# The last query tile turned on TensorE, and y weighted on VectorE, in a two-layer hybrid block

## The chip, the core and the metric

The kernel runs on one core of a Trainium2 chip. The time is the time on the device in microseconds, the median of the runs of one program. The engines of a core work through queues of their own and meet at semaphores: TensorE (PE, with its weight loads as PEld), VectorE (DVE), ScalarE (ACT), GpSimd (POOL), and SyncE (SP), which only issues DMAs here.

## The reference

Two blocks follow each other over 256 tokens of width 1024, each with two layers; all arithmetic is in fp32. The change touches the first block's layers. In one such layer the normalised input is multiplied by a wide matrix, and its columns are cut into z, x, B, C, dt, q, k, v and two gates. A state-space mixer makes y from x, B, C and dt; a windowed attention takes q (three patterns of eight heads), k and v; both results go through a matrix of their own and are gated and added.

```python
y = ssd_chunked(xs, dt, a, bm, cm) + d_skip.astype(f32)[:, None] * xs
y = y.reshape(bsz, s, SSD_INNER) * jax.nn.silu(z.astype(f32))
yg = y.reshape(bsz, s, SSD_GROUPS, SSD_INNER // SSD_GROUPS)
yg = yg * lax.rsqrt(jnp.mean(yg * yg, axis=-1, keepdims=True) + RMS_EPS)
return (yg.reshape(bsz, s, SSD_INNER) * norm_w.astype(f32)).astype(z.dtype)
...
q = apply_partial_rope(q.reshape(bsz, s, ATTN_N_PAT, ATTN_KV_HEADS, ATTN_HEAD_DIM), cos, sin)
k = apply_partial_rope(k.reshape(bsz, s, ATTN_KV_HEADS, ATTN_HEAD_DIM), cos, sin)
...
scores = jnp.einsum("brhnqe,brhnke->brhnqk", qb, kb, preferred_element_type=jnp.float32) * (dh ** -0.5)
...
merged = (jax.nn.sigmoid(g_ssd) * (y_ssd @ w_ssd_branch[layer])
          + jax.nn.sigmoid(g_attn) * (y_attn @ w_attn_branch[layer]))
```

## The kernel before

**Products.** fp32 weights are split into a high part (`WH`, rounded by ScalarE, line 1170) and a low part (`WL`, the difference, by VectorE, line 1694, the helper `tt` of every VectorE sum, difference and product of two tiles). The activations are split likewise (`uH`, `uL` and `bH`, `bL`). A product is then three matmuls, high by high, high by low and low by high (lines 673 to 675, or 927 to 929 where the result is wanted with columns on the partitions).

**Chunks.** Weights come in chunks of 128 x 2048 in a ring of three buffers. A layer of the first block has one list of chunks: 0 to 47 are the 24 tiles of the wide matrix, two chunks each (tile i has chunks 2i and 2i + 1), then come the branch matrices. A tile of 512 columns takes 24 matmuls a chunk. Every engine has a loop over the chunk number c, and all other work is hung into these loops by hand: "if c == ...". So each engine has a fixed order, and a number c stands for a different moment on each: ScalarE and VectorE split chunk c when TensorE has finished chunk c - 3, so their turn c is at about the time of TensorE's chunk c - 2. In front of its chunk c TensorE runs the small work of turn c (the function `before`).

**Turning the q and k tiles.** The tiles k0, q0, q2, q4, k1, q1, q3, q5 (tiles 3, 7, 10, 13, 17, 19, 20, 21) come out with tokens on the partitions and are wanted with the head's elements there. ScalarE takes the tile out of PSUM into `ev[...]` (line 1298), VectorE applies the rope (turn 2i + 5), POOL lays the upper and lower halves of the words apart (line 1651), SP issues a DMA transpose of 2-byte elements (line 578), and ScalarE merges the halves again into `qT` or `kT` (line 1315, two instructions, at the turns `QK_MERGE`). The semaphore `qk_out` counts finished tiles. TensorE waits for four of them before the scores of heads 0 to 3 (turns 36 to 42) and for all eight before those of heads 4 to 7 (from turn 48, line 814).

**The heads.** Head n has its scores at turn `HEAD_AT[n]` on TensorE (banks 4 to 6), mask, exponentials and normalisation on VectorE and ScalarE two and three turns on, a DMA turn of the probabilities, and the product with the values at turn `HEAD_AT[n] + 4` (lines 711 and 712, bank 7 for heads 0 to 5). ScalarE takes the high part out of bank 7 (line 1356) and VectorE the low part, which raises `o_ready`, both at turn `HEAD_AT[n] + 6`. For head 3 these turns are 42, 46 and 48.

**The y groups.** y comes in four groups of 512 columns, from the x tiles 2, 5, 8 and 11. For group g with x tile i: TensorE turns the conv tile at turn 2i + 5 (line 678, eight transposes), which waits for the convolution's silu and for the last sum of y of the group before (`ssd_y`); y is finished, gated and scaled at turns 2i + 11 to 2i + 13; POOL, a DMA transpose and POOL again turn it; and at turn 2i + 16 it is weighted with the norm's columns and split: ScalarE writes four high parts (line 1350, scaled by a column), VectorE four low parts (line 1958). `xpad` and `conv` are the tiles of the convolution, whose twelve steps on VectorE have line 1780; the turns of its two halves are 2i + 4 and 2i + 5. `EM` (the profile calls it ssd_decay) holds the decay masks, `scratch` is the large region that holds qT, y, ev and most else.

Of the kernel before, what the change touches and what calls it, by code (L numbers as in the profile page):

```python
# [16 lines left out]
F32 = mybir.dt.float32  # L17
# [126 lines left out]
def build(nc, stream, pars, const1, const2, onehot, relb, final_g, ple_g, w_x, out, rev):  # L144
    ctx = ExitStack()
    with ctx:
# [63 lines left out]
        def words(name, at_col, shape):  # L210
# [33 lines left out]
                   words("qk_halves6", BTOK_AT, [2 * T * 512])[:, :], words("qk_halves7", BTOK_AT + 1024, [2 * T * 512])[:, :]]  # L244
# [3 lines left out]
                   early("qk_turned6", 1, 20, 2 * T * 512, U16)[:, :], early("qk_turned7", 0, 20, 2 * T * 512, U16)[:, :]]  # L248
# [128 lines left out]
        words_split = signal("words_split", 8 + GROUPS)  # L377
        words_turned = [signal("words_turned0", 16 * 6), signal("words_turned1", 16 * 6)]
# [34 lines left out]
        y_high = signal("y_high", GROUPS)  # L413
# [30 lines left out]
        y_scaled = signal("y_scaled", GROUPS)  # L444
        conv_done = signal("conv_done", 6)
# [80 lines left out]
        QK_SPLIT = (12, 20, 26, 32, 42, 44, 46, 47)  # L526
        QK_TURN, Y_TURN = (0, 2, 4, 6, 8, 9, 10, 11), (1, 3, 5, 7)
        QK_MERGE = (14, 24, 30, 34, 46, 47, 48, 49)
        CONV_AT = 4
        Y_HIGH, Y_LOW = 16, 16  # L530
# [140 lines left out]
        def _(pe):  # L671
# [42 lines left out]
            def before(l, c):  # L714
# [78 lines left out]
                for g, i in enumerate(XT):  # L793
# [8 lines left out]
                    if c == 2 * i + 10:  # L802
                        pe.wait_ge(ssd_exp.sem, ssd_exp.at(l, 2 * g + 2))
                        nc.tensor.matmul(ps[:, 7, :], BC[:, 4 + g, tok(1)], state, start=True, stop=True).then_inc(off_ps.sem, 1)  # L804
                for n, s in enumerate(HEAD_AT):
# [353 lines left out]
        def _(act):  # L1159
# [32 lines left out]
            for l in range(L):  # L1192
# [39 lines left out]
                for c in range(4, CHUNKS1):  # L1232
# [73 lines left out]
                    for n in range(8):  # L1306
                        if c == QK_MERGE[n]:
# [10 lines left out]
                            ins.then_inc(qk_out.sem, 1)  # L1318
                    for g, i in enumerate(XT):
# [26 lines left out]
                        if c == 2 * i + Y_HIGH:  # L1346
                            act.wait_ge(y_whole.sem, y_whole.at(l, g + 1))
                            for j in range(4):
                                jj = 4 * g + j
                                ins = nc.scalar.activation(bH[:, jj, :].rearrange("p (t n) -> p t n", t=T), Y[g % 2][:, :, tok(j)],  # L1350
                                                           ACT.Identity, scale=par[:, C_SN + jj:C_SN + jj + 1])
                            ins.then_inc(y_high.sem, 1)
# [251 lines left out]
        def _(pool):  # L1604
# [6 lines left out]
            for l in range(L):  # L1611
# [7 lines left out]
                def lay_apart(n):  # L1619

                    pool.wait_ge(att_p.sem, att_p.at(l, n + 1))
                    if n == 4:
                        pool.wait_ge(qk_out.sem, qk_out.at(l, 8))
# [13 lines left out]
                for n in range(8):  # L1637
# [6 lines left out]
                    if 5 <= n < 7:  # L1644
                        lay_apart(n - 3)
# [3 lines left out]
                    if n >= 6:  # L1649
                        pool.wait_ge(qk_out.sem, qk_out.at(l, n - 1))  # L1650
                    nc.gpsimd.tensor_copy(qk_half[n].rearrange("p (h n) -> p h n", h=2),
                                          words_of(ev[QK[n][2]]).rearrange("p n h -> p h n")).then_inc(words_split.sem, 1)
                    if n < GROUPS:
                        g, m = n, Y_TURN[n]
                        pool.wait_ge(y_scaled.sem, y_scaled.at(l, g + 1))
                        if g == 2:
# [5 lines left out]
                                              y_back[g].rearrange("p (h m) -> p h m", h=2)).then_inc(y_whole.sem, 1)  # L1662
                for n in range(4, 7):
                    lay_apart(n)
                    put_together(n)
# [24 lines left out]
        def _(dve):  # L1690
# [102 lines left out]
            for l in range(L):  # L1793
# [49 lines left out]
                for c in range(4, CHUNKS1):  # L1843
# [67 lines left out]
                    for g, i in enumerate(XT):  # L1911
# [32 lines left out]
                        if c == 2 * i + 13:  # L1944
# [4 lines left out]
                            ins.then_inc(y_scaled.sem, 1)  # L1949
                    for n, i in enumerate((0, 1) + XT):  # L1950
                        if c in (2 * i + CONV_AT, 2 * i + CONV_AT + 1):
                            convolve(l, n, c - 2 * i - CONV_AT)
                    for g, i in enumerate(XT):
                        if c == 2 * i + Y_LOW:
                            dve.wait_ge(y_high.sem, y_high.at(l, g + 1))
                            for j in range(4):
                                jj = 4 * g + j
                                ins = nc.vector.scalar_tensor_tensor(
                                    out=bL[:, jj, :].rearrange("p (t n) -> p t n", t=T), in0=Y[g % 2][:, :, tok(j)],
# [431 lines left out]
```

## Time and profile before

| | |
|---|---|
| median of 3 runs | 1525.48 us (1525.25 to 1525.74) |
| profiled execution | 1525.48 us |
| its span | 1523.7 us |
| busy: TensorE matmuls, VectorE, ScalarE, POOL | 1508.5, 1039.7, 926.4, 179.9 us |
| DMA | 288.08 MB, 189 GB/s on the mean |

The span reaches from the first to the last instruction of the profile; the execution is 1.78 us longer. Matmuls overlap, so a row of x8 shows the time from the first's start to the last's end, and starts are what is to be compared. A number in square brackets behind a row is idle time in front of it and what ended it. Times of rows are from the start of the span, and unless it is said otherwise they lie in the first of the two layers of the first block, which begins at 0; the second one repeats it from about 596 us on.

### The profile page before, as it was taken

Reading aid. Unit: us, or ns where it says so; the run is one execution under the profiler, and the core shown is the slowest. Engines: PE = TensorE matmul, PEld = TensorE weight load, DVE = VectorE, ACT = ScalarE, POOL = GpSimd, SP = SyncE. Lnnn points to the kernel's source line nnn. Section 1 sums busy time; section 2 is a strip of 40 time slices with the busy share of each in tenths; the row PEclk is TensorE's granted clock in tenths of the full one; section 3 lists DMA queues with packets and bytes.
Section 4 is the critical chain, followed back from the end, with each engine's and each line's share of the span. In section 5 each row is a group of like instructions: output and inputs, shape, how many; then the busy total and the mean of one; then the engine's idle time right before and its main releaser. Section 6 shows DMA issues by size and latency. Waiting matters only on the chain.

```text
span 1523.7 us, 18981 instructions
## 1 busy us (share of the span) xinstructions
PE 1508.5 (99%) x7612; PEld 1276.1 (84%) x7612; DVE 1039.7 (68%) x1324; ACT 926.4 (61%) x1118; POOL 179.9 (12%) x115
## 2 busy tenths in 40 slices
PE   7999999999999999999999999999999999999998
PEld 7888888888888888988888888888888878888887
DVE  6978876756665555787887775665545676677665
ACT  5766787574355553667778565436555565666564
POOL 1001121422000100001102231100010020002000
PEclk9999999999999999999999999999999999999999
DMA  7456655775456774445556685537767584448541
GB/s 275 166 166 181 194 183 185 203 215 175 167 199 212 204 235 173 171 164 181 177 181 196 189 223 185 169 138 242 221 166 254 212 256 169 149 148 246 174 152 65
DMA packets 132399, 288.08 MB, mean 189 GB/s; under 512 B 97079, under 2 KB 98008, under 8 KB 101848
## 3 DMA queue, kind: packets, MB, share of 16 engines
q1 hardware_dynamic: 131208, 284.44, 58.6%
q10 hardware_dynamic: 1104, 2.43, 0.5%
q8 instruction: 60, 0.98, 0.3%
q14 instruction: 27, 0.22, 0.0%
HBM read 261.69 MB, written 1.84 MB: 173 GB/s over the span
## 4 chain that ended last, share of the span: by engine, by line
PE 93%; DVE 5%; ACT 1%; issue 1%; DMA 0%; SPq 0%; ACTq 0%; DVEq 0%
PE ps L673 25%; PE ps L675 25%; PE ps L674 25%; PE ps L678 2%; PE ps L927 2%; PE ps L928 2%; PE ps L929 2%; DVE w_low L1694 2%; PE ps L799 2%; PE ps L814 1%; DVE conv L1780 1%; PE ps L816 1%; ACT w_high L1170 1%; PE ps L786 0%; PE ps L804 0%
## 5 line engine op out<-in xcount | busy, mean ns | idle before, releaser
L1694 DVE TENSOR_TENSOR w_low<-w_raw,w_high 128x2048 fp32r<-128x2048 f32 (+1 forms) x250 | 574.7, 2299 | 369.0 <-ACT w_high L1170 302.0
L673 PE MATMUL ps<-w_high,u_high 128*128 128x512 f32 x1376 | 547.4, 398 | 0.5 <-DVE w_low L1694 0.5
L675 PE MATMUL ps<-w_high,u_low 128*128 128x512 f32 x1376 | 536.8, 390 | 0.0
L674 PE MATMUL ps<-w_low,u_high 128*128 128x512 f32 x1376 | 535.9, 389 | 0.0
L1170 ACT ACTIVATE w_high<-w_raw 128x2048 fp32r<-128x2048 f32 (+1 forms) x196 | 369.2, 1884 | 260.0 <-PE ps L675 246.8
L673 PEld LDWEIGHTS ps<-w_high,u_high 128*128 128x128 f32 x1376 | 258.5, 188 | 55.4 <-issue 2.4
L675 PEld LDWEIGHTS ps<-w_high,u_low 128*128 128x128 f32 x1376 | 258.3, 188 | 55.0
L674 PEld LDWEIGHTS ps<-w_low,u_high 128*128 128x128 f32 x1376 | 258.7, 188 | 53.9 <-issue 2.4
L673 PE MATMUL ps<-w_high,b_high 128*128 128x512 f32 x384 | 151.5, 395 | 0.0
L675 PE MATMUL ps<-w_high,b_low 128*128 128x512 f32 x384 | 149.7, 390 | 0.0
L674 PE MATMUL ps<-w_low,b_high 128*128 128x512 f32 x384 | 149.5, 389 | 0.0
L1418 ACT ACTIVATE w_high<-w_raw 128x2048 fp32r<-128x2048 f32 x50 | 95.3, 1910 | 45.8 <-PE ps L675 45.6
L927 PE MATMUL ps<-u_high,w_high 128*128 128x256 f32 x384 | 112.8, 294 | 4.2 <-DVE w_low L1694 3.9
L928 PE MATMUL ps<-u_low,w_high 128*128 128x256 f32 x384 | 109.3, 285 | 0.0
L929 PE MATMUL ps<-u_high,w_low 128*128 128x256 f32 x384 | 109.2, 284 | 0.0
L1694 DVE TENSOR_TENSOR scratch<-scratch 128x128 f32<-128x128 f32 (+3 forms) x156 | 68.3, 471 | 34.5 <-ACT scratch L1361 27.1
L675 PEld LDWEIGHTS ps<-w_high,b_low 128*128 128x128 f32 x384 | 72.1, 188 | 15.2
L674 PEld LDWEIGHTS ps<-w_low,b_high 128*128 128x128 f32 x384 | 72.2, 188 | 14.4
L673 PEld LDWEIGHTS ps<-w_high,b_high 128*128 128x128 f32 x384 | 72.1, 188 | 14.3
L927 PEld LDWEIGHTS ps<-u_high,w_high 128*128 128x128 f32 x384 | 74.3, 194 | 6.7 <-DVE w_low L1694 4.3
L928 PEld LDWEIGHTS ps<-u_low,w_high 128*128 128x128 f32 x384 | 74.3, 194 | 1.7 <-issue 1.4
L929 PEld LDWEIGHTS ps<-u_high,w_low 128*128 128x128 f32 x384 | 74.3, 193 | 0.0
(241 smaller groups left out, 1513.1 us busy)
## 6 DMA issues: line engine op xcount, KB each, us to landing
w_raw<-in_stream SPq DMA_DIRECT2D x238, 1024.0 KB, 4.9
w_raw<-in_stream SPq DMA_DIRECT2D x12, 512.0 KB, 4.1
par<-in_pars SPq DMA_DIRECT2D x4, 269.0 KB, 5.2
h<-in_x SPq DMA_DIRECT2D x4, 256.0 KB, 4.9
ple_gain<-in_ple_g ACTq DMA_DIRECT2D x2, 512.0 KB, 5.6
out<-h SPq DMA_DIRECT2D x4, 256.0 KB, 2.1
scratch<-in_const SPq DMA_DIRECT2D x1, 768.0 KB, 7.6
rev<-scratch ACTq DMA_DIRECT2D x1, 768.0 KB, 3.6
```

The lines of the kernel that those rows point to most:

```text
L673: nc.tensor.matmul(o, hi, whi, start=start, stop=False, **kw)
L674: nc.tensor.matmul(o, hi, wlo, start=False, stop=False, **kw)
L675: return nc.tensor.matmul(o, lo, whi, start=False, stop=stop, **kw)
L678: return nc.tensor.transpose(o, i, ident)
L799: last = nc.tensor.matmul(ps[:, 4 + t, e * HD:(e + 1) * HD], EM[t][:, e, :], xdt[:, t, e * HD:(e + 1) * HD], start=True, stop=True)
L814: nc.tensor.matmul(ps[:, 4 + g // 2, (g % 2) * S:(g % 2 + 1) * S], qT[:, g, hh, tok(1)], kT[:, hh, :], start=True, stop=True)
L927: nc.tensor.matmul(o, WH[:, slot, w], uH[:, kk, :], start=first, stop=False, skip_group_check=True)
L928: nc.tensor.matmul(o, WH[:, slot, w], uL[:, kk, :], start=False, stop=False, skip_group_check=True)
L929: last = nc.tensor.matmul(o, WL[:, slot, w], uH[:, kk, :], start=False, stop=kk == KD - 1, skip_group_check=True)
L1170: nc.scalar.activation(WH[:, c % RING, 0:n], W[:, c % RING, 0:n], ACT.Copy).then_inc(high_ready, 1)
L1418: nc.scalar.activation(WH[:, n % RING, :], W[:, n % RING, :], ACT.Copy).then_inc(high_ready, 1)
L1694: return nc.vector.tensor_tensor(out=o, in0=a, in1=b, op=op)
```

## The change

Two edits. First, q5, the last of the eight tiles, isn't turned by POOL, DMA and merge any more. TensorE turns it in front of chunk 47 (`QK_LAST`) with eight fp32 transposes into banks 6 and 7, and ScalarE copies both banks into `qT` at turn 49, in the place of the last merge. TensorE waits there for the rope of q5 (`roped`) and for the low part of head 3's output (the fourth `o_ready`), since that output lies in bank 7. Second, y is weighted in place by VectorE, token half by token half, then ScalarE copies the half to `bH` (rounding it) and VectorE subtracts it into `bL`. This stands ahead of the mask products and of the next convolution's first half in VectorE's turn; the old low parts stood behind them.

```diff
-        QK_SPLIT = (12, 20, 26, 32, 42, 44, 46, 47)
-        QK_TURN, Y_TURN = (0, 2, 4, 6, 8, 9, 10, 11), (1, 3, 5, 7)
-        QK_MERGE = (14, 24, 30, 34, 46, 47, 48, 49)
+        QK_SPLIT = (12, 20, 26, 32, 42, 44, 46)
+        QK_TURN, Y_TURN = (0, 2, 4, 6, 8, 9, 10), (1, 3, 5, 7)
+        QK_MERGE = (14, 24, 30, 34, 46, 47, 48)
+        QK_LAST = 47
         CONV_AT = 4
-        Y_HIGH, Y_LOW = 16, 16
+        Y_WEIGH = 16
...
+                if c == QK_LAST:
+                    pe.wait_ge(roped.sem, roped.at(l, 8))
+                    pe.wait_ge(o_ready.sem, o_ready.at(l, 4))
+                    for hh in range(4):
+                        for t in range(T):
+                            last = turn(ps[:, 6 + hh // 2, (hh % 2) * S + t * P:(hh % 2) * S + (t + 1) * P], ev[QK[7][2]][:, t, tok(hh)])
+                    last.then_inc(qk_ps.sem, 1)
...
-                    for n in range(8):
+                    for n in range(7):
                         if c == QK_MERGE[n]:
...
+                    if c == 49:
+                        act.wait_ge(qk_ps.sem, qk_ps.at(l, 1))
+                        nc.scalar.activation(qT[:, 2], ps[:, 6:8, :].rearrange("p b (j s) -> p (b j) s", j=2), ACT.Copy)\
+                            .then_inc(qk_out.sem, 1)
...
-                        if c == 2 * i + Y_HIGH:
-                            act.wait_ge(y_whole.sem, y_whole.at(l, g + 1))
-                            for j in range(4):
-                                jj = 4 * g + j
-                                ins = nc.scalar.activation(bH[:, jj, :].rearrange("p (t n) -> p t n", t=T), Y[g % 2][:, :, tok(j)],
-                                                           ACT.Identity, scale=par[:, C_SN + jj:C_SN + jj + 1])
-                            ins.then_inc(y_high.sem, 1)
+                        if c == 2 * i + Y_WEIGH:
+                            for t in range(T):
+                                act.wait_ge(y_weighted.sem, y_weighted.at(l, 2 * g + t + 1))
+                                nc.scalar.activation(bH[:, 4 * g:4 * g + 4, tok(t)], four(Y[g % 2][:, t, :]), ACT.Copy)\
+                                    .then_inc(y_high.sem, 1)
...
                     if n == 4:
-                        pool.wait_ge(qk_out.sem, qk_out.at(l, 8))
+                        pool.wait_ge(qk_out.sem, qk_out.at(l, 6))
...
-                for n in range(8):
+                for n in range(7):
...
+                        if c == 2 * i + Y_WEIGH:
+                            dve.wait_ge(y_whole.sem, y_whole.at(l, g + 1))
+                            for t in range(T):
+                                tt(four(y[:, t, :]), four(y[:, t, :]),
+                                   bc(par[:, C_SN + 4 * g:C_SN + 4 * g + 4].unsqueeze(2), 4, P), ALU.mult).then_inc(y_weighted.sem, 1)
+                            for t in range(T):
+                                dve.wait_ge(y_high.sem, y_high.at(l, 2 * g + t + 1))
+                                tt(bL[:, 4 * g:4 * g + 4, tok(t)], four(y[:, t, :]), bH[:, 4 * g:4 * g + 4, tok(t)].bitcast(F32),
+                                   ALU.subtract).then_inc(y_ready.sem, 1)
...
-                    for g, i in enumerate(XT):
-                        if c == 2 * i + Y_LOW:
-                            dve.wait_ge(y_high.sem, y_high.at(l, g + 1))
-                            for j in range(4):
-                                jj = 4 * g + j
-                                ins = nc.vector.scalar_tensor_tensor(
-                                    out=bL[:, jj, :].rearrange("p (t n) -> p t n", t=T), in0=Y[g % 2][:, :, tok(j)],
-                                    scalar=par[:, C_SN + jj:C_SN + jj + 1],
-                                    in1=bH[:, jj, :].bitcast(F32).rearrange("p (t n) -> p t n", t=T), op0=ALU.mult, op1=ALU.subtract)
-                            ins.then_inc(y_ready.sem, 2)
```

VectorE's order at its turn 20 in a layer (the split of chunk 20 to that of chunk 21), before; `tt` has line 1694 in the old file and 1706 in the new one:

```order
L1694 TENSOR_TENSOR w_low<-w_raw,w_high 128x2048
L1937 COPY ssd_decay_57<-scratch 128x8
L1694 TENSOR_TENSOR ssd_decay_57<-ssd_decay_57,scratch 128x8x127
L1694 TENSOR_TENSOR xpad<-ps,rinv_rows 128x4x256
L1958 SCALAR_TENSOR_TENSOR b_low<-scratch,par,b_high 128x256 x4
L1694 TENSOR_TENSOR scratch<-scratch,ps 128x512
L1694 TENSOR_TENSOR w_low<-w_raw,w_high 128x2048
```

The same place in the changed kernel:

```order
L1706 TENSOR_TENSOR w_low<-w_raw,w_high 128x2048
L1706 TENSOR_TENSOR scratch<-scratch,par 128x512 x2
L1706 TENSOR_TENSOR b_low<-scratch,b_high 128x4x128 x2
L1949 COPY ssd_decay_57<-scratch 128x8
L1706 TENSOR_TENSOR ssd_decay_57<-ssd_decay_57,scratch 128x8x127
L1706 TENSOR_TENSOR xpad<-ps,rinv_rows 128x4x256
L1706 TENSOR_TENSOR scratch<-scratch,ps 128x512
```

Two products and two differences now stand in front of the mask products and of xpad; the four low parts behind xpad are gone.

ScalarE's order around its turns 48 and 49, before (line 1315 merges q3 and then q5, line 1356 is the high part of head 3's output):

```order
L1170 ACTIVATE w_high<-w_raw 128x2048
L1298 ACT_TABLE_LOAD
L1298 ACTIVATE scratch<-ps,small 128x512 x2
L1315 ACTIVATE scratch<-qk_turned_80 128x2x4x128 x2
L1356 ACTIVATE b_high<-ps 128x256
L1170 ACTIVATE w_high<-w_raw 128x2048
L1315 ACTIVATE scratch<-qk_turned_81 128x2x4x128 x2
```

And in the changed kernel:

```order
L1180 ACTIVATE w_high<-w_raw 128x2048
L1308 ACT_TABLE_LOAD
L1308 ACTIVATE scratch<-ps,small 128x512 x2
L1325 ACTIVATE scratch<-qk_turned_79 128x2x4x128 x2
L1368 ACTIVATE b_high<-ps 128x256
L1180 ACTIVATE w_high<-w_raw 128x2048
L1331 ACTIVATE scratch<-ps 128x1024
```

The order up to the high part is the same; only the last merge has become a copy out of two banks.

TensorE in front of chunk 47 in the changed kernel, where the old one goes from matmul to matmul:

```order
L678 MATMUL ps<-w_high,u_low 128x512
L681 MATMUL ps<-con,scratch 128x128 x8
L676 MATMUL ps<-w_high,u_high 128x512
L677 MATMUL ps<-w_low,u_high 128x512
```

This is the only row that TensorE has gained in a layer.

## Rows read from the trace of the kernel before

**Rows 1.** The page: busy time of the engines, and the chain that ended last.
```profile
PE 1508.5 (99%) x7612; PEld 1276.1 (84%) x7612; DVE 1039.7 (68%) x1324; ACT 926.4 (61%) x1118; POOL 179.9 (12%) x115
...
PE 93%; DVE 5%; ACT 1%; issue 1%; DMA 0%; SPq 0%; ACTq 0%; DVEq 0%
```

**Rows 2.** Waits of TensorE: total us, times, longest.
```profile
PE ps L678 <- DMA con<-in_const: 3.9, 1, 3.9
```

**Rows 3.** Timeline of TensorE, conv transposes of group 2: start us, length us.
```profile
151.98 1.03 PE L678 MATMUL ps<-con,conv 128*128 128x128 f32 x8
152.77 0.48 PE L673 MATMUL ps<-w_high,u_high 128*128 128x512 f32 x1
153.09 0.40 PE L674 MATMUL ps<-w_low,u_high 128*128 128x512 f32 x1
```

**Rows 4.** TensorE in one stretch: busy (count), granted clock, DMA share, GB/s.
```profile
314.00:319.25 5.25, 5.25 (x24) 1.00 0.92 270
```

**Rows 5.** Timeline of TensorE: the first matmul of chunk 47.
```profile
319.30 0.39 PE L673 MATMUL ps<-w_high,u_high 128*128 128x512 f32 x1
```

**Rows 6.** Timeline of ScalarE at its turn 48.
```profile
313.41 1.91 ACT L1170 ACTIVATE w_high<-w_raw 128x2048 fp32r<-128x2048 f32 x1 [1.05 <-PE ps L675]
315.35 1.28 ACT L1298 ACT_TABLE_LOAD   x1
316.64 1.27 ACT L1298 ACTIVATE scratch<-ps,small 128x512 f32<-128x512 f32 x2
317.80 2.56 ACT L1315 ACTIVATE scratch<-qk_turned 128x1024 uint16<-128x1024 uint16 x2
320.22 0.36 ACT L1356 ACTIVATE b_high<-ps 128x256 fp32r<-128x256 f32 x1
```

**Rows 7.** Timeline of VectorE: end of q5's rope, and head 3's low part.
```profile
313.45 0.49 DVE L1694 TENSOR_TENSOR scratch<-scratch 128x128 f32<-128x128 f32 x2
...
320.61 0.43 DVE L1694 TENSOR_TENSOR b_low<-ps,b_high 128x256 fp32r<-128x256 f32 x1 [2.56 <-ACT b_high L1356]
```

**Rows 8.** Timeline of TensorE: chunk 47 ends, scores of head 4.
```profile
324.51 0.39 PE L675 MATMUL ps<-w_high,u_low 128*128 128x512 f32 x1
324.90 0.70 PE L814 MATMUL ps<-scratch 128*128 128x256 f32 x2
...
325.66 0.60 PE L814 MATMUL ps<-scratch 128*128 128x256 f32 x2
```

**Rows 9.** Timeline of VectorE from its turn 20 to the last sum of y.
```profile
137.53 0.17 DVE L1937 COPY ssd_decay<-scratch 128x8 f32<-128x8 f32 x1
...
139.98 1.67 DVE L1958 SCALAR_TENSOR_TENSOR b_low<-scratch,par,b_high 128x256 fp32r<-128x256 f32 x4
141.58 0.68 DVE L1694 TENSOR_TENSOR scratch<-scratch,ps 128x512 f32<-128x512 f32 x1
...
150.69 0.69 DVE L1694 TENSOR_TENSOR scratch<-scratch 128x512 f32<-128x512 f32 x1
```

**Rows 10.** Groups by form: count, busy us, mean ns, idle before.
```profile
L1694 DVE TENSOR_TENSOR scratch<-scratch 128x512 f32<-128x512 f32 x36 | 24.7, 692 | 6.3 <-ACT scratch L1466 5.2
L1694 DVE TENSOR_TENSOR b_low<-scratch,b_high 128x512 fp32r<-128x512 f32 x22 | 15.1, 684 | 0.0
...
L1407 ACT ACTIVATE b_high<-scratch 128x512 fp32r<-128x512 f32 x22 | 13.5, 614 | 0.0
```

**Rows 11.** Timeline of TensorE in the first 15 us of the run.
```profile
9.75 0.58 PE L927 MATMUL ps<-u_high,w_high 128*128 128x256 f32 x1 [3.85 <-DVE w_low L1694]
...
10.77 0.41 PE L928 MATMUL ps<-u_low,w_high 128*128 128x256 f32 x1
10.98 0.41 PE L929 MATMUL ps<-u_high,w_low 128*128 128x256 f32 x1
...
14.12 0.28 PE L928 MATMUL ps<-u_low,w_high 128*128 128x256 f32 x1
14.23 0.29 PE L929 MATMUL ps<-u_high,w_low 128*128 128x256 f32 x1
```

More of the change, by code:

```diff
@@ L243, in build @@
                    words("qk_halves4", BTOK_AT, [2 * T * 512])[:, :], words("qk_halves5", BTOK_AT + 1024, [2 * T * 512])[:, :],
-                   words("qk_halves6", BTOK_AT, [2 * T * 512])[:, :], words("qk_halves7", BTOK_AT + 1024, [2 * T * 512])[:, :]]
+                   words("qk_halves6", BTOK_AT, [2 * T * 512])[:, :]]
         qk_turn = [early("qk_turned0", 0, 4, 2 * T * 512, U16)[:, :], early("qk_turned1", 1, 4, 2 * T * 512, U16)[:, :],
@@ L247, in build @@
                    early("qk_turned4", 1, 20, 2 * T * 512, U16)[:, :], early("qk_turned5", 0, 20, 2 * T * 512, U16)[:, :],
-                   early("qk_turned6", 1, 20, 2 * T * 512, U16)[:, :], early("qk_turned7", 0, 20, 2 * T * 512, U16)[:, :]]
+                   early("qk_turned6", 1, 20, 2 * T * 512, U16)[:, :]]
         y_half = [words("y_halves0", E_AT, [2 * T * 512])[:, :], words("y_halves1", E_AT, [2 * T * 512])[:, :],
@@ L376, in build @@
         off_ps = signal("off_ps", GROUPS)
-        words_split = signal("words_split", 8 + GROUPS)
-        words_turned = [signal("words_turned0", 16 * 6), signal("words_turned1", 16 * 6)]
+        qk_ps = signal("qk_ps", 1)
+        words_split = signal("words_split", 7 + GROUPS)
+        words_turned = [signal("words_turned0", 16 * 6), signal("words_turned1", 16 * 5)]
         y_whole = signal("y_whole", GROUPS)
@@ L412, in build @@
         group_root = signal("group_root", GROUPS)
-        y_high = signal("y_high", GROUPS)
+        y_high = signal("y_high", 2 * GROUPS)
         qk_out = signal("qk_out", 8)
@@ L444, in build @@
         y_scaled = signal("y_scaled", GROUPS)
+        y_weighted = signal("y_weighted", 2 * GROUPS)
         conv_done = signal("conv_done", 6)
@@ L1643, in _ @@
                         put_together(n - 4)
-                    if 5 <= n < 7:
                         lay_apart(n - 3)
@@ L1648, in _ @@
                         pool.wait_ge(state_out.sem, state_out.at(l, GROUPS))
-                    if n >= 6:
-                        pool.wait_ge(qk_out.sem, qk_out.at(l, n - 1))
+                    if n == 6:
+                        pool.wait_ge(qk_out.sem, qk_out.at(l, 5))
                     nc.gpsimd.tensor_copy(qk_half[n].rearrange("p (h n) -> p h n", h=2),
@@ L1662, in _ @@
                                               y_back[g].rearrange("p (h m) -> p h m", h=2)).then_inc(y_whole.sem, 1)
+                put_together(3)
                 for n in range(4, 7):
```

## The prediction

> **What bounds the kernel now.** I read the busy shares and the chain that ended last first: TensorE is busy for 1508.5 of 1523.7 us, and the chain lies on it for 93% [rows 1]. Then the waits of TensorE alone, to see what it still waits for: the longest are one of 3.9 us for the constants and one of 3.9 us for the first weights [rows 2, 11], both in the first ten microseconds of the run, and nothing in the middle of a layer comes near them. So the rest of the work (ScalarE and VectorE splitting weights, POOL and the DMA turning tiles) is hidden behind matmuls. A saving on those engines is worth nothing by itself. Two things can move the time: instructions added to or taken from TensorE, and a result that now arrives later than TensorE reaches the instruction that wants it. For the second, the places where the change touches a semaphore were read engine by engine in the timeline: the start of chunk 47 and of chunk 48, and the start of chunk 21, each as "when is TensorE there, when is the result there". A chunk of 24 matmuls takes about 5.3 us here: 24 of them lie between 314.00 and 319.25 [rows 4].
>
> **Part 1: eight transposes on TensorE, per layer.** They have the form of the eight that turn a conv tile. Those start at 151.98 and the next matmul starts at 152.77, so eight cost 0.79 us; the matmul behind them is followed by its neighbour after 0.32 us, where 0.23 us is usual (23 steps from 319.30 to 324.51, [rows 5, 8]), which is 0.09 more [rows 3]. 0.88 us a layer, 1.76 us for two. They stand in front of a matmul on the engine that bounds, so nothing hides them. From below 0.79; from above, if they didn't overlap at all: seven starts 0.11 apart and one full length make the 1.03 us of the row, so one is about 0.26 long, and eight of them 2.1 us a layer.
>
> **Part 2: what TensorE waits for in front of them.** The eight write banks 6 and 7, and bank 7 holds the output of head 3 until VectorE has split it, so the code waits for the rope of q5 and for the fourth o_ready. The rope is done at 313.94, long before [rows 7]. The fourth o_ready is the end of the split of head 3, from 320.61 to 321.04. TensorE starts chunk 47 at 319.30 [rows 5], when the 24 matmuls of chunk 46 are issued. VectorE cannot do the split earlier, since it sits idle for 2.6 us until ScalarE has made the high part, and ScalarE works through its queue from 313.41 to 320.58 without a pause: weights of chunk 48, a table load, the tile ga0, the merge of q3, and only then the high part of head 3 [rows 6]. Its first item is released by the end of chunk 45 on TensorE, so this queue doesn't start earlier by being left alone, and the change takes nothing out of it. With 0.03 us from end to start (320.58 to 320.61), TensorE gets going at 321.07 instead of 319.30: 1.77 us. In layer 1 the same two rows stand at the same distance, so one pair is shown for both. A restart after a wait costs about 0.10 more: the first pair of L814, which did wait, took 0.70 us, the next pair 0.60 [rows 8]. So 1.87 us a layer, 3.74 us for two. Before, the same o_ready was wanted only by the value product of head 4 at chunk 52, five chunks later. Behind the waiting transposes stands all of chunk 47, and everything that is released by its matmuls; as TensorE is the bound, that is a shift of the whole program. Bounds: nothing, if ScalarE's queue were 1.8 us shorter in this place; 3.3 us a layer if TensorE had to wait out the whole merge (2.56 us, [rows 6]) once more.
>
> **Part 3: what is given back at chunk 48.** The scores of head 4 waited for the last merge: the last matmul of chunk 47 starts at 324.51, the next should follow after 0.23 us and starts at 324.90, 0.16 us late, and the pair takes 0.10 us more than its neighbour [rows 8]. 0.26 us a layer, 0.52 us for two, goes: the two merges are replaced by one copy of 1024 columns out of PSUM, and a pair of 512 columns each out of PSUM takes 1.27 us [rows 6]. ScalarE is free of the weights of chunk 49 by about 322.4, the transposes end at about 322.1, so q5 is in place at about 323.7, and TensorE reaches the scores at about 327.4. The last DMA turn on the SP queue, POOL's laying apart ahead of it and the waits for both go too; nobody on TensorE waited for them beyond those 0.16 us, so I cost them at nothing. The loads behind them on SP may only come earlier.
>
> **Part 4: the weighting of y.** Before, ScalarE multiplies and rounds (four instructions), and VectorE multiplies again and subtracts at the end of its turn at chunk 20 (four instructions, 139.98 to 141.65, the next from 141.58: 1.60 us) [rows 9]. Now VectorE multiplies (two of 0.69 us), ScalarE copies (two of 0.61), VectorE subtracts (two of 0.68) [rows 10], and this stands at the front of the turn, before the masks of the second half. On VectorE neighbours overlap by about 0.07 (141.65 against 141.58). From 137.53: multiplications end at 138.22 and 138.83, ScalarE's copies at 138.87 and 139.47, the subtractions start at 138.90 and 139.50, and what was next at 137.53 is next at 140.10: 2.57 us later. Taking off the 1.60 us that stood further back leaves +0.97 us. From there to 151.38 VectorE has no pause longer than a hand-over, so the last sum of y, which ends at 151.38 [rows 9], ends at 152.35. TensorE wants it (ssd_y) for the transposes of the next conv tile, which start at 151.98 [rows 3]: 0.60 us of slack, and 0.97 + 0.03 us of delay. 0.40 us late, with the restart 0.50. This happens where y of one group is weighted in the turn in which a conv tile begins: for two of the four groups, in both layers, four times, 2.0 us. The slack reads 0.60 in the other three places too; one of the four stands in the rows. In the turns at chunks 32 and 38 no conv tile follows, and nothing that TensorE takes next from VectorE is as close. Below: 0, if the hand-overs go faster by 0.4 us. Above: 2.57 + 0.03 - 0.60 + 0.10 = 2.1 us each, 8.4 us, if nothing came back from the four instructions that go. I take the worked-out 2.0, with less trust than in parts 1 and 2.
>
> The sum: 1.76 + 3.74 - 0.52 + 2.0 = 7.0 us. The profiled execution took 1525.48 us, 1.78 more than its span, and it equals the median of the three runs, so 1525.5 + 7.0 = 1532.5 us, 0.46% slower. I forecast 1532.4. (A measurement of this kernel can't tell less than about 0.2%, 3 us, from no change.)
>
> **The clock, a rule that speaks against the change.** At the start of the run TensorE had stood still for 3.85 us; the matmuls of 256 columns then followed each other every 0.21 us (1.2 GHz), and from 14.12 on every 0.12 us (2.4 GHz) [rows 11]. So it kept the lower pace for some 4.3 us. In the new kernel the engine stands idle 1.8 us and then only transposes for 0.9 us, twice. If it fell for 4.3 us each time, half the work of that stretch would be lost, 2.1 us a time, 4.3 us in all. The Trainium skill (TensorE: Matmul & The Clock Gate, "HAM oscillation") holds that waits repeated between short bursts of matmuls bring the clock down to half and warns against them, and its part on the PE-mode transpose adds that transposes don't count as activity. No stretch of this trace with such a wait in the middle of dense work shows it either way.
>
> **The rivals.**
> A, the y chain stays hidden: parts 1 to 3 alone, +5.0 us, 1530.5. For it: the slack is 0.60 and my excess 0.40, of hand-overs that I estimate. Against it: VectorE has no idle time on that stretch to take it up.
> B, the y chain costs more: +1 us at each of the four places instead of 0.5, 9.0 us, 1534.5. For it: ScalarE's weights of chunk 21 are now behind its two copies, and the conv tile's first products behind those; against: by the same reckoning each still ends before the step that wants it.
> C, the clock falls in chunk 47: 7.0 + 4.3 = 11.3 us, 1536.8.
> D, not slower: the wait for o_ready is not paid. That is so if ScalarE makes the high part of head 3 by about 318.8; it decides on one number, the 1.77 us. Then 1.76 - 0.52 = 1.2 us remain, with the y chain 3.2; 1526.7 to 1528.7, mostly no change. For it: only if the merge of q3 or the table load went, and both are still in the new order. Faster than before would need a gain of which the waits of TensorE show at most 0.5 us.
>
> **Chances.** The forecast 0.56 (own range 1531.2 to 1534.0), A 0.16, B 0.09, C 0.08, D 0.11. Slower by over 0.2% are the first four (0.89) and a sliver of D, 0.90; within 0.2%: most of D, 0.08; faster: 0.02. The range reaches from just below A to where B ends and C begins: 1529.6 to 1535.8.
>
> **What would show it.** In the new profile: a wait of TensorE at the transposes with scratch for an input, released by VectorE's split of head 3, 1.8 us, twice; behind it eight transposes in 0.8 to 0.9 us; no wait in front of the scores of head 4; a wait of 0.3 to 0.5 us in front of the conv transposes of groups 2 and 3, absent at groups 0 and 1; 16 more matmuls on TensorE and no other change of their count. The sum is wrong if o_ready comes before 319.3 in that stretch, if the y block takes less than 2.2 us on VectorE, or if matmuls behind the wait are spaced like those at the start.

## The result, and the profile after

The changed kernel takes 1533.44 us (1533.17 to 1533.92) against 1525.48 before: slower, ratio 1.0051 with a 95% interval of 1.0038 to 1.0064. Its profiled execution took 1532.54 us with a span of 1530.7, so it stands 7.06 us above the profiled execution of before, where the sum was 7.0. By the medians the difference is 7.96 us; the profiled execution is the fastest of the eight that were taken of the changed kernel, which reach up to 1533.92. The busy shares hardly move; the chain does. The page of the changed kernel, TensorE's busy time and the chain that ended last:

```profile
PE 1510.8 (99%) x7628; PEld 1277.3 (83%) x7628; DVE 1043.2 (68%) x1324; ACT 919.3 (60%) x1100; POOL 178.5 (12%) x113
...
PE 86%; DVE 9%; ACT 3%; issue 1%; DMA 0%; ACTq 0%; DVEq 0%
```

TensorE has the 16 matmuls more that were added, and only 2.3 us more of busy time. But the chain now leaves it for VectorE and ScalarE for 12% of the span, where it was 6% [rows 1]. Which results are late, the waits of TensorE say (total us, times, longest):

```profile
PE ps L681 <- DVE b_low L1706: 3.4, 2, 1.7
PE ps L681 <- DVE scratch L1706: 2.2, 6, 0.4
```

Ahead of them stand only the two of the start of the run, as before [rows 2, 11]. The first here is new, once a layer. The second is the wait of transposes (L681 is `turn`, L678 before) for sums of VectorE; four of its six are new. The first in the timeline of TensorE (start us, length us):

```profile
319.89 0.39 PE L678 MATMUL ps<-w_high,u_low 128*128 128x512 f32 x1
321.98 1.06 PE L681 MATMUL ps<-con,scratch 128*128 128x128 f32 x8 [1.71 <-DVE b_low L1706]
322.80 0.48 PE L676 MATMUL ps<-w_high,u_high 128*128 128x512 f32 x1
323.12 0.39 PE L677 MATMUL ps<-w_low,u_high 128*128 128x512 f32 x1
...
328.13 0.39 PE L678 MATMUL ps<-w_high,u_low 128*128 128x512 f32 x1
328.37 0.59 PE L824 MATMUL ps<-scratch 128*128 128x256 f32 x2
```

From the last matmul of chunk 46 to the first transpose are 2.10 us by the unrounded times, and a step without a wait is 0.23: 1.87 us lost. Of these 1.71 are the lateness of head 3's low part, the rest is the hand-over to TensorE. The transposes occupy 0.82 us, and the matmul behind them is followed by its neighbour after 0.32 us instead of 0.23: 0.91 us. And the scores of head 4 (L824) follow the last matmul after 0.24 us and the pair takes 0.59, where it was 0.39 and 0.70 [rows 8]: 0.26 us given back. ScalarE's queue, which sets the moment of the wait, and VectorE's answer:

```profile
314.23 1.91 ACT L1180 ACTIVATE w_high<-w_raw 128x2048 fp32r<-128x2048 f32 x1 [1.05 <-PE ps L678]
316.16 1.28 ACT L1308 ACT_TABLE_LOAD   x1
317.46 1.27 ACT L1308 ACTIVATE scratch<-ps,small 128x512 f32<-128x512 f32 x2
318.61 2.54 ACT L1325 ACTIVATE scratch<-qk_turned 128x1024 uint16<-128x1024 uint16 x2
321.01 0.37 ACT L1368 ACTIVATE b_high<-ps 128x256 fp32r<-128x256 f32 x1
321.27 1.91 ACT L1180 ACTIVATE w_high<-w_raw 128x2048 fp32r<-128x2048 f32 x1
323.08 1.03 ACT L1331 ACTIVATE scratch<-ps 128x1024 f32<-128x1024 f32 x1
```

```profile
321.41 0.42 DVE L1706 TENSOR_TENSOR b_low<-ps,b_high 128x256 fp32r<-128x256 f32 x1 [2.94 <-ACT b_high L1368]
```

It is the queue of [rows 6] 0.8 us further on, item for item. The copy of q5 out of the two banks (L1331) ends at 324.11, over four microseconds before the scores want it.

The other place, VectorE from its turn 20 to the last sum of y, and TensorE at the conv transposes behind it:

```profile
137.15 1.29 DVE L1706 TENSOR_TENSOR scratch<-scratch,par 128x512 f32<-128x512 f32 x2
138.54 1.30 DVE L1706 TENSOR_TENSOR b_low<-scratch,b_high 128x512 fp32r<-128x512 f32 x2
139.75 0.17 DVE L1949 COPY ssd_decay<-scratch 128x8 f32<-128x8 f32 x1
...
151.33 0.69 DVE L1706 TENSOR_TENSOR scratch<-scratch 128x512 f32<-128x512 f32 x1
```

```profile
151.38 0.39 PE L678 MATMUL ps<-w_high,u_low 128*128 128x512 f32 x1
152.16 1.06 PE L681 MATMUL ps<-con,conv 128*128 128x128 f32 x8 [0.40 <-DVE scratch L1706]
```

The block takes 139.75 - 137.15 = 2.60 us. The turn began 0.38 us earlier on the clock of the run than before (137.15 against 137.53) and its last sum starts 0.64 later (151.33 against 150.69, [rows 9]): 1.02 us of delay. The transposes start 0.79 us behind the last matmul instead of 0.23: 0.56 us. In the transposes themselves 0.03 us more are lost, since the second follows the first after 0.14 us instead of 0.11. The same gap, 0.79, stands at 192.5, 750.9 and 792.0; at group 1 there was nothing to wait for, 0.23 (110.89 to 111.12).

### The profile page after: what moved, and what is told of

It is laid out like the page before. It is cut to its first block, busy times and chain, and to the rows that moved or that the text cites. A ratio compares the mean times of both kernels' runs of the same rounds, so it can differ in the third digit from the quotient of the medians.

```text
span 1530.7 us, 18991 instructions
## 1 busy us (share of the span) xinstructions
PE 1510.8 (99%) x7628; PEld 1277.3 (83%) x7628; DVE 1043.2 (68%) x1324; ACT 919.3 (60%) x1100; POOL 178.5 (12%) x113
## 4 chain that ended last, share of the span: by engine, by line
PE 86%; DVE 9%; ACT 3%; issue 1%; DMA 0%; ACTq 0%; DVEq 0%
PE ps L676 23%; PE ps L678 23%; PE ps L677 23%; DVE w_low L1706 3%; PE ps L681 3%; DVE conv L1792 2%; PE ps L937 2%; PE ps L939 2%; PE ps L938 2%; PE ps L824 1%; DVE scratch L1706 1%; ACT w_high L1180 1%; PE ps L802 1%; PE ps L826 1%; DVE xpad L1706 1%
## 5 line engine op out<-in xcount | busy, mean ns | idle before, releaser
L678 PE MATMUL ps<-w_high,u_low 128*128 128x512 f32 x1376 | 537.0, 390 | 0.0
L678 PEld LDWEIGHTS ps<-w_high,u_low 128*128 128x128 f32 x1376 | 258.3, 188 | 55.1
L678 PE MATMUL ps<-w_high,b_low 128*128 128x512 f32 x384 | 149.8, 390 | 0.0
L678 PEld LDWEIGHTS ps<-w_high,b_low 128*128 128x128 f32 x384 | 72.1, 188 | 15.2
```

Source lines behind the costliest of these rows:

```text
L678: return nc.tensor.matmul(o, lo, whi, start=False, stop=stop, **kw)
```

## How the experiments are read

Since every kernel here issues the same products in the same order, each one's TensorE timeline can be laid over that of before, matmul by matmul. How far it lags behind after each place gives each place's cost in that one execution, apart from the first 23 us, where the profiled executions differ by up to 1.5 us although the kernels don't differ there. All numbers in us, counted from TensorE's first matmul (3.9 to 4.1 us after the span begins); "chunk 47" is the wait, the transposes and what the scores give back. The medians are a second reading beside the places. The two need not agree closely: the intervals of the ratios are 2.6 to 4.7 us wide.

| kernel | first 23 us | conv transposes, 4 places | L802, 2 places | chunk 47, each layer | elsewhere | end | median (runs) | ratio to before |
|---|---|---|---|---|---|---|---|---|
| changed kernel | -0.41 | 0.6, 0.6, 0.6, 0.6 | 0 | 2.52, 2.54 | 0 | +7.05 | 1533.44 (5) | 1.0051 [1.0038, 1.0064] |
| e_first | +0.62 | 0 | 0 | 2.53, 2.53 | 0 | +5.68 | 1532.09 (5) | 1.0038 [1.0025, 1.0050] |
| e_second | +0.21 | 0.6, 0.6, 0.6, 0.6 | 0 | 0, 0 | 0 | +2.62 | 1527.91 (11) | 1.0016 [1.0007, 1.0025] |
| e_banks | -0.22 | 0.6, 0.6, 0.6, 0.6 | 0 | 0.63, 0.63 | 0.12 | +3.56 | 1529.05 (11) | 1.0022 [1.0013, 1.0030] |
| e_late | -0.73 | 0 | 0.53, 0.54 | 2.53, 2.53 | 0 | +5.45 | 1531.51 (5) | 1.0037 [1.0025, 1.0050] |
| e_both | +1.53 | 0 | 0.57, 0.53 | 0.63, 0.63 | 1.62 | +5.55 | 1528.01 (10) | 1.0016 [1.0006, 1.0025] |
| e_twice | -0.64 | 0 | 0.53, 0.59 | 1.50, 1.50 | 1.61 | +5.08 | 1530.54 (7) | 1.0029 [1.0018, 1.0040] |
| e_long | -0.29 | 0.6, 0.6, 0.6, 0.6 | 0 | 8.60, 7.90 | 0 | +18.54 | 1543.09 (4) | 1.0112 [1.0097, 1.0128] |
| e_free | -0.83 | 0 | 0 | 0.63, 0.63 | 0 | +0.54 | 1527.55 (11) | 1.0011 [1.0002, 1.0020] |

The kernel before, run beside them on the same chip, took 1525.48 (with the changed kernel), 1525.60 (e_first, e_second, e_banks, e_both), 1525.84 (e_late, e_twice, e_long) and 1526.24 (e_free); these three groups of experiments ran on three chips. One execution of e_both that took 6656.55 us is left out. In the changed kernel the start hid 0.41 us: its places cost 7.46.

## One edit at a time: e_first and e_second

e_first makes the first edit only. The weighting of y is put back:

```diff
-        Y_WEIGH = 16
+        Y_HIGH, Y_LOW = 16, 16
...
+                        if c == 2 * i + Y_HIGH:
+                            act.wait_ge(y_whole.sem, y_whole.at(l, g + 1))
```

> The first edit alone: q5 is turned on TensorE, y is weighted as before. Theory (the three terms stand by themselves): +5.0 us over the kernel before, of which 3.7 is the wait for head 3's split, 1.8 the transposes, and 0.5 comes back at the scores; the starts at the conv transposes of groups 2 and 3 are 0.23 us behind the matmul before, as before. Rival (the edits act on each other, for instance since POOL and the DMA queue are emptier): the conv transposes still start late, and the whole is 7 to 8 us.

Its waits of TensorE that matter here:

```profile
PE ps L680 <- DVE b_low L1707: 3.4, 2, 1.7
...
PE ps L680 <- DVE scratch L1707: 0.6, 2, 0.3
```

The wait for b_low is whole, the one for the sums of y is back to the 0.6 us of the kernel before. 2.53 us a layer, 5.06 in all, where 5.0 was expected. The medians differ by 6.5 us (by the interval 3.8 to 7.6), 1.4 more than the places of the one profile account for; no run shows where that stands.

e_second makes the second edit only: q5 goes by POOL, DMA and merge again.

```diff
-        QK_MERGE = (14, 24, 30, 34, 46, 47, 48)
-        QK_LAST = 47
+        QK_MERGE = (14, 24, 30, 34, 46, 47, 48, 49)
```

> The second edit alone: y is weighted on VectorE, q5 is turned by DMA as before. Theory: +2.2 us (four times 0.56 us of wait in front of the conv transposes of groups 2 and 3), and the 0.16 us of wait at the scores of head 4 stay. Rival (the y block is hidden and its 2 us come from something that the first edit triggers): within 0.5 us of the kernel before.

```profile
PE ps L679 <- DVE scratch L1693: 2.2, 6, 0.4
```

Of the two new waits only this one is there: 0.6 us at four places, 2.4 us. 5.06 and 2.40 make the 7.46 of the changed kernel, so by the places the two edits act apart from each other, and both cost.

## What the first edit's 2.5 us are: e_banks, e_twice

e_banks puts the transposes into banks 4 and 5. These are free once the scores of head 3 have been masked, long before chunk 47, so TensorE waits for that and not for the output in bank 7 (ScalarE's copy reads banks 4 and 5 too):

```diff
-                    pe.wait_ge(o_ready.sem, o_ready.at(l, 4))
+                    pe.wait_ge(att_masked.sem, att_masked.at(l, 4))
...
-        last = turn(ps[:, 6 + hh // 2, ...
+        last = turn(ps[:, 4 + hh // 2, ...
```

> The changed kernel, with the eight transposes into banks 4 and 5 instead of 6 and 7, so that they wait for the mask of head 3, long done, and not for the split of head 3's output. Theory (bank 7 is what TensorE waits for): 3.7 us less than the changed kernel, +3.3 us over the kernel before; no wait in front of the transposes. Rival (TensorE would wait there for something else that comes as late, or the time goes to the next place where ScalarE is behind): less than 2 us of it comes back.

TensorE, and ScalarE's high part of head 3, in e_banks:

```profile
320.08 0.40 PE L678 MATMUL ps<-w_high,u_low 128*128 128x512 f32 x1
320.32 1.04 PE L681 MATMUL ps<-con,scratch 128*128 128x128 f32 x8
321.11 0.47 PE L676 MATMUL ps<-w_high,u_high 128*128 128x512 f32 x1
```

```profile
321.24 0.37 ACT L1368 ACTIVATE b_high<-ps 128x256 fp32r<-128x256 f32 x1
```

The high part is as late as ever, a microsecond behind the first transpose, and nobody waits. The transposes follow after 0.24 us, occupy 0.79, and the matmul behind them costs 0.09 more. With the 0.26 given back, 0.63 us a layer remain of 2.53; the difference, 1.90, is the wait and the 0.03 us that the first transpose behind it took longer. Both layers show it. (The 0.12 us under "elsewhere" stand at the value products of one head in layer 1.) So the wait comes from the choice of the bank, not from the transposes.

e_twice (the kernel e_both, below, with every transpose of q5 issued twice) sizes the transposes by themselves:

```diff
-                    for hh in range(4):
+                    for hh in tuple(range(4)) * 2:
```

> As the kernel with banks 4 and 5 and the later weighting, but each of the eight transposes is done twice. Theory (a transpose in front of a chunk costs its own 0.11 us of TensorE and nothing else): 8 more in each layer are 0.87 us a layer, +1.75 us over the kernel without the doubling, +3.0 over the kernel before; 16 of them stand in a row 0.11 us apart. Rival (part of the 0.88 us is a fixed price of the switch from one kind of matmul to the other): less than 1.4 us more; or (they don't overlap) 4 us more.

```profile
319.31 1.91 PE L681 MATMUL ps<-con,scratch 128*128 128x128 f32 x16
320.97 0.48 PE L676 MATMUL ps<-w_high,u_high 128*128 128x512 f32 x1
```

Sixteen occupy 1.66 us where eight took 0.79: 0.87 us for eight more, and the place costs 1.50 instead of 0.63. So the doubling costs 1.74 us over both layers, as expected (1.75): in front of chunk 47 the length of the transposes on TensorE is paid in full.

## What the second edit's 2.4 us are: e_late, e_both, e_free

e_late is the changed kernel with the y blocks of groups 0 and 1 two turns later, away from the turn in which a conv tile begins (they stood at 20, 26, 32 and 38):

```diff
-        Y_WEIGH = 16
+        Y_WEIGH = (22, 28, 32, 38)
...
-                        if c == 2 * i + Y_WEIGH:
+                        if c == Y_WEIGH[g]:
```

> The changed kernel, banks 6 and 7 as they are, with groups 0 and 1 of y weighted two turns later (22 and 28 instead of 20 and 26): the same instructions in another place. Theory (it is the place on VectorE's way to the last sum of y that costs): 2.2 us less than the changed kernel, +4.9 over the kernel before, and the conv transposes start 0.23 us behind the matmul before. Rival (the amount of work costs, wherever it stands): the time stays within 0.5 us of the changed kernel's, with the waits in another place.

Its waits of TensorE:

```profile
PE ps L681 <- DVE b_low L1706: 3.4, 2, 1.7
...
PE ps L681 <- DVE scratch L1706: 0.6, 2, 0.3
PE ps L802 <- DVE ssd_decay L1706: 0.5, 2, 0.3
```

The four waits are gone, so they did come from the block's place. But a wait of another kind has come, at the products of xdt with the decay masks, and costs 0.53 us a layer, nearly half of the gain of 1.2; 4.9 us over the kernel before had been expected, and the places add up to 6.1. Why is read on VectorE, POOL and TensorE at turn 32, where the block of group 2 stands, which e_late did not move:

```profile
215.11 3.42 DVE L1706 TENSOR_TENSOR w_low<-w_raw,w_high 128x2048 fp32r<-128x2048 f32 x1 [1.58 <-ACT w_high L1180]
218.46 2.98 DVE L1706 TENSOR_TENSOR scratch<-scratch,par 128x512 f32<-128x512 f32 x2
...
222.81 1.21 DVE L1706 TENSOR_TENSOR ssd_decay<-ssd_decay,scratch 128x1016 f32<-128x1016 f32 x1
```

```profile
216.35 3.94 POOL L1662 COPY qk_halves<-scratch 128x2048 uint16<-128x2048 uint16 x1
```

```profile
224.08 2.00 PE L802 MATMUL ps<-xdt,ssd_decay 128*128 128x64 f32 x16 [0.27 <-DVE ssd_decay L1706]
```

The two products take 2.98 us instead of 1.29: they end 1.14 us after POOL's copy (220.29), so nearly all of their own work lies behind it. The decay mask, which now stands behind the block, is done at 224.02, and TensorE, that was due at 223.65 (0.23 behind the last matmul, which starts at 223.42), starts at 224.08. With the slower restart that is the 0.53. In the changed kernel it came to the same place at 225.10, 1.2 us of that lag from the two waits before, and the mask was there with 0.2 us to spare. One wait had hidden the next.

e_both joins e_banks and e_late.

> The changed kernel with banks 4 and 5, and with groups 0 and 1 of y weighted two turns later (22 and 28 instead of 20 and 26), behind the last sum of y that the conv transposes wait for. Theory: only the transposes are left, 1.8 us, less 0.5 at the scores: +1.2 us over the kernel before, no wait of TensorE in either place. Rival (work on VectorE and ScalarE costs time wherever it stands, through other queues): over 2.5 us remain.

It has the same two waits at L802 and 0.63 us a layer at chunk 47; of the 7.46 us, 2.36 are left (2.4 by the medians), twice the 1.2 that were expected, since no wait at L802 had been foreseen. Its profiled execution shows 1.62 us more at one other place, told in the last section. e_free then moves group 2's block too:

```diff
-        Y_WEIGH = (22, 28, 32, 38)
+        Y_WEIGH = (22, 28, 34, 38)
```

> The kernel e_both with the y weighting of group 2 at turn 34 instead of 32 (groups 0 and 1 at 22 and 28, group 3 at 38, as in e_both); the transposes of q5 into banks 4 and 5. In e_both and e_late TensorE has a new wait of 0.3 us, once a layer, at the products of xdt with the decay masks (L802), which costs 0.53 us each. My theory: it comes from group 2's y block at turn 32, whose two products on VectorE take 2.98 us instead of 1.29 because a copy of POOL (3.9 us) runs beside them, and which stands in front of the mask product that makes the decay tile. In the changed kernel itself the two waits of groups 0 and 1 (0.6 us each) had hidden it. Then without it at turn 32 the wait at L802 is gone and the total is 1.06 us less than in e_both: the eight transposes alone, 2 x 0.63 = 1.3 us over before, 1526.8 us. Rival 1: the wait at L802 comes from groups 0 and 1 being later (turns 22 and 28), then it stays as it is, 1527.9. Rival 2: the block at turn 34 makes something else late, a new wait elsewhere, 1527.4 to 1529.

VectorE and POOL at turn 32, and TensorE, in e_free:

```profile
218.29 1.86 DVE L1949 COPY ssd_decay<-scratch 128x8 f32<-128x8 f32 x1
220.06 1.21 DVE L1706 TENSOR_TENSOR ssd_decay<-ssd_decay,scratch 128x1016 f32<-128x1016 f32 x1
```

```profile
216.20 3.92 POOL L1662 COPY qk_halves<-scratch 128x2048 uint16<-128x2048 uint16 x1
```

```profile
223.45 1.89 PE L802 MATMUL ps<-xdt,ssd_decay 128*128 128x64 f32 x16
```

No wait: group 2's block was the cause, and rivals 1 and 2 of that run fall. POOL's copy still holds VectorE up (a copy of eight columns takes 1.86 us), but nothing late stands behind it. What is left of the change is 2 x 0.63 us, the price of the transposes on the engine that bounds; the medians differ by 1.31, though their interval, 0.3 to 3.1 us, is too wide to call this more than agreement. No version beats the kernel before: behind the start of the run, the waits of TensorE that the profile of e_free lists are the ones of the kernel before.

## The clock: e_long

The changed kernel stands idle for 1.87 us more in front of its transposes, and the clock does not move. e_long lengthens the idle time to see whether it can fall here at all, or the gap was too short. Two activations of one column, each with another table, stand in front of ScalarE's merge of q3:

```diff
+                            if n == 6:
+                                nc.scalar.activation(spare[:, 2:3], spare[:, 1:2], ACT.Exp)
+                                nc.scalar.activation(spare[:, 3:4], spare[:, 1:2], ACT.Sqrt)
```

> The changed kernel, with an exponential and a root of one column on ScalarE ahead of q3's merge, which bring two table loads, about 3.0 us, in front of the high part of head 3. Theory (TensorE waits for exactly that queue): the gap in front of the eight transposes grows from 2.1 to 5.1 us in each layer, and the time by 6.0 us, to 1539.5. The rule on the clock: a gap of 5 us, longer than the 3.85 us at the start, makes the matmuls behind it run 0.43 us apart instead of 0.23 for some microseconds, and the time grows by a further 2 to 4 us. The other side: no matmul behind the gap is slower, and no more than 6.0 us are added.

TensorE in e_long around chunk 47:

```profile
325.27 1.94 PE L681 MATMUL ps<-con,scratch 128*128 128x128 f32 x8 [4.71 <-DVE b_low L1709]
...
328.29 0.63 PE L676 MATMUL ps<-w_high,u_high 128*128 128x512 f32 x1
328.72 0.63 PE L677 MATMUL ps<-w_low,u_high 128*128 128x512 f32 x1
...
331.27 0.39 PE L677 MATMUL ps<-w_low,u_high 128*128 128x512 f32 x1
```

And in stretches (length, busy time of PE, PEld, DVE, ACT and POOL, granted clock, DMA share, GB/s), with the changed kernel's below it:

```profile
324.00:328.00 4.00, 2.73 (x11) 2.56 (x12) 1.92 (x2) 3.22 (x4) 0.00 (x0) 0.55 0.00 0
328.00:332.00 4.00, 4.00 (x13) 3.10 (x12) 0.79 (x1) 0.27 (x1) 0.00 (x0) 0.59 0.51 168
332.00:336.00 4.00, 4.00 (x21) 3.43 (x20) 0.00 (x0) 1.25 (x1) 0.00 (x0) 1.00 0.22 94
```

```profile
320.00:324.00 4.00, 2.29 (x15) 1.87 (x14) 1.21 (x2) 4.00 (x4) 0.00 (x0) 1.00 0.62 248
```

The wait grows by the 3.0 us that the two table loads and activations take on ScalarE (1.28 and 0.20 us each). Behind it the transposes occupy 1.59 us instead of 0.82 (the next matmul starts at 326.86), and the matmuls follow each other every 0.43 us, 1.2 GHz, until 331.27. So this place costs 8.60 us: the 2.52 of the changed kernel, 3.0 of wait and 3.1 of clock; in layer 1 it is 2.4 of clock. The profiled execution is the slowest of the four. By the medians, each taken over the kernel before on its own chip, e_long costs 17.25 us and the changed kernel 7.96; of the 9.3 us between them 6.0 are wait, so over all executions the clock took some 1.6 us a layer. The fall that the prediction weighed does happen in this kernel, and it takes one wait in the middle of dense work, no repetition: after an idle time of 4.7 us the clock fell, after one of 1.7 us it did not, twice each. Idle times between the two were not tried. Transposes alone did not bring it down: e_twice issues sixteen in a row (1.66 us), and the matmul behind them is followed at the full pace. Rival C had a price near the measured one (2.1 us a time) and the wrong gap.

## Why the prediction was right, step by step

- **Part 1, the transposes, 0.88 us a layer.** Right: 0.91 in the changed kernel, 0.87 by doubling them. The conv transposes of before [rows 3] were the right row.
- **Part 2, the wait, 1.87 us a layer.** Right (1.87), and from the cause named: with another bank it is gone, and 1.90 us a layer with it. The agreement to the hundredth is luck: the low part was 1.71 us late and not 1.74, and the hand-over took 0.15 and not 0.13. The upper bound given there is a slip in the sum: 1.87 and once more the merge's 2.56 are 4.4 us a layer, not 3.3. What made it readable was that the first item of ScalarE's queue hangs on chunk 45 of TensorE itself [rows 6], so the queue moves with TensorE and the distance stays.
- **Part 3, given back, 0.26 us a layer.** Right, 0.26: 0.15 to 0.16 of the gap and the rest of the pair. (A chunk takes 24 steps of 0.227 us, 5.44 and not the 5.3 read off [rows 4]; no term of the sum used it.) The earlier DMA turn and POOL's work were indeed worth nothing.
- **Part 4, y, 0.50 us at four places.** The right places, and 0.6 each instead of 0.50 (0.56 in the gap, 0.03 in the transposes): the term of the sum that was too small, by 0.4 us in all. The block took 2.60 us, not 2.57, and the last sum was 1.02 late, not 0.97. e_late shows that the place was the cause. The bound above, 8.4 us, was far off, since the four instructions that went did give their time back.
- **Part 4, the sentence on the turns at chunks 32 and 38.** It held for the changed kernel, where nothing is paid there, but for a thinner reason than it gave. The slack at turn 32 before is 3.2 us, the block with POOL's copy beside it and its new place ahead of the mask took 3.0 of them net of TensorE's own lag, and what remained was 0.2 us. I had cost the block at its usual 2.57 without looking at what POOL does there; e_late and e_free found it.
- **The rivals.** A falls (the four places do cost). B falls: 0.6, not 1. C falls for this gap. D, the wait not paid, falls too; what it would have looked like is e_banks. The time alone would not have told the forecast from B: the median, 1533.44, lies halfway between 1532.4 and 1534.5. The places do.
- **The sum.** 7.46 us at the places, less 0.41 of the start in that execution, is the 7.05 measured; I had 7.0 and took no account of the start. So that the profiled executions differ by 7.06 is in part luck: y's 0.4 too little and the start's 0.41 cancel. The medians differ by 7.96, which the interval of the ratio (5.8 to 9.8 us) allows; where the 0.5 us above the places' 7.46 stand, no run shows.

## What to carry to other kernels

When work is moved onto the engine that bounds, its own length is paid in full, but the larger price can be the buffer it is given: choose the one whose last reader is done long before, not the nearest in the code, and read the moment of that reader's end from the trace. A block that is put ahead of others in an engine's turn must be followed to each consumer behind it, with what the neighbouring engine does in each of the turns. And when a wait is removed, look for the one that it hid: the lag that it caused had made the next result look early.

## What the runs showed of the hardware that was not expected

**VectorE and POOL stand still for each other, in turn.** A copy of 128x8 on VectorE takes 0.17 us, and 1.86 us in e_free at 218.29, where it ends with POOL's copy, within 0.05 us (218.29 + 1.86 = 220.15 against 216.20 + 3.92 = 220.12). That copy of POOL is itself held up. Here are one of the same size that has POOL's usual length, in the kernel before, and, in e_free, VectorE's instruction and POOL's copy ahead of those two:

```profile
307.48 1.89 POOL L1651 COPY qk_halves<-scratch 128x2048 uint16<-128x2048 uint16 x1 [5.11 <-ACT scratch L1315]
```

```profile
214.92 3.45 DVE L1706 TENSOR_TENSOR w_low<-w_raw,w_high 128x2048 fp32r<-128x2048 f32 x1 [1.58 <-ACT w_high L1180]
```

```profile
213.76 2.52 POOL L1672 COPY scratch<-y_turned 128x2048 uint16<-128x2048 uint16 x1 [4.44 <-DMA y_turned<-y_halves]
```

POOL's first copy ends at 216.28; VectorE's difference of 2048 columns, which usually takes 2.3 us, ends 2.09 us after it, at 218.37; POOL's second copy ends 1.75 us after that, at 220.12; and VectorE's small copy right behind. The same distances, 2.09 and 1.75, stand in the kernel before (the ends are 216.07, 218.16, 219.91 and 219.94), so the small copy is held there too, and in e_late, where the pair of products took 2.98 instead of 1.29 us. Instructions of VectorE that read one operand in PSUM and one in SBUF are not held: four of 512 columns beside POOL's copy at 117.69 in the kernel before take 0.68 us each. The Trainium skill (SBUF — State Buffer, "SBUF: two separate sides") says that VectorE and GpSimd share a pair of ports as an exclusive lock for a whole instruction, that whoever starts first has it, and that the other blocks fully; the trace agrees, in both directions. It names instructions of VectorE with two inputs in SBUF or in a two-port mode, and counts a copy of fp32 within SBUF to the latter, which would cover the small copy; its mode is not visible in any trace here.

**The clock can fall without an idle gap.** In the second block TensorE runs four products over 33 rows (L1040, eight records) in 2.84 us, in all these kernels. In two of the ten profiled executions, e_both's and e_twice's, the matmuls behind them then ran at half pace for some 3 us and cost 1.6 us; in the other profiles they did not. The stretches of e_both:

```profile
1225.00:1228.00 3.00, 3.00 (x10) 1.62 (x10) 2.79 (x6) 0.30 (x2) 0.00 (x0) 1.00 0.79 322
1228.00:1231.00 3.00, 3.00 (x8) 2.32 (x8) 0.00 (x0) 3.00 (x4) 0.00 (x0) 0.54 0.75 246
```

and of e_banks:

```profile
1228.00:1231.00 3.00, 3.00 (x15) 2.44 (x14) 0.15 (x1) 3.00 (x4) 0.00 (x0) 1.00 0.80 273
```

TensorE was busy throughout in both. What decides it was not tried, and that the 33 rows have to do with it is a guess from where the fall stands. The eleven executions of e_second lie in two heaps, eight at 1527.4 to 1528.1 us and three at 1529.95 to 1530.3. A fall of this kind may be behind it, but the heaps lie 2.4 us apart and not 1.6, and the one execution with a profile is of the lower heap.

**The first 23 us vary.** They took 0.83 us less to 1.53 us more than in the profile of before, in kernels that don't differ there. In e_both TensorE waited 4.4 us for the first weights, in the changed kernel 3.7 and in the kernel before 3.9. The rest comes mostly from when the clock rises: TensorE's steps shorten from the 1.2 GHz to the 2.4 GHz pace at about 14.1 us in the kernel before, at 13.5 in the changed one, 12.6 in e_free and 16.6 in e_both. Differences under a microsecond between single executions of this kernel mean nothing until that is taken off, and the alignment matmul by matmul does it.
